# The mixing product in two halves of its sum, the first beside the masked attention

## What is computed

```python
h = rms_norm(x, mix_norm_g)
(lru_x, lru_z, ml_u, ml_o, ml_z, ml_i, ml_f,
 mo_q, mo_k, mo_v, mo_z) = jnp.split(h @ w_in, SPLIT_POINTS, axis=-1)
y_lru = rg_lru_branch(...)                      # 512 wide
y_ml = mlstm_branch(...)                        # 768 wide, 4 heads
# masked attention, 6 heads of 128, with linear biases; 768 wide
y_mo = softmax(q k^T * scale - slope * distance, causal) v * silu(mo_z)
x = x + concatenate([y_lru, y_ml, y_mo]) @ w_out        # the mixing product
x = x + memory_cross_attention(rms_norm(x), rms_norm(mem))
```

## Time and profile before

| what | value |
|---|---|
| median of 3 runs | 1984.25 us (1982.85 to 1990.74) |
| the profiled execution's own time | 1982.04 us |
| its span, first to last instruction | 1980.2 us |
| mean granted TensorE clock | 0.953 |
| busy: PE, PEld | 1813.0, 1547.3 us |
| busy: DVE, ACT | 1434.6, 805.5 us |
| read from memory | 307 MB, 156 GB/s over the span |

### The profile page before, as it was taken

How to read it: one execution, slowest core, us unless ns; L and a number is a source line. 1 busy time by engine, 2 the same in 40 slices (tenths; PEclk the granted TensorE clock), 3 DMA queues, 4 the chain that set the end, 5 groups by cost and what they waited for, 6 DMA issues and landing times. The chain is left out here.

```text
span 1980.2 us, 26887 instructions
## 1 busy us (share of the span) xinstructions
PE 1813.0 (92%) x10559; PEld 1547.3 (78%) x10559; DVE 1434.6 (72%) x2250; ACT 805.5 (41%) x1268; POOL 7.2 (0%) x18
## 2 busy tenths in 40 slices
PE   7999988997799887999999989997989999999797
PEld 6899988885688766878887867785978976666597
DVE  5788768787799767878687869776772677777444
ACT  6544364634244534233332223223453444444343
POOL 1000000000000000000000000000000000000000
PEclk9999999997899888999999999998999999999898
DMA  6588745443577333345454546552342443433252
GB/s 211 188 263 264 234 127 160 128 133 119 188 247 255 128 108 117 106 160 177 132 197 158 194 131 214 188 191 91 121 150 74 142 165 114 139 111 114 73 184 89
DMA packets 168998, 311.09 MB, mean 157 GB/s; under 512 B 14908, under 2 KB 23464, under 8 KB 168872
## 3 DMA queue, kind: packets, MB, share of 16 engines
q1 hardware_dynamic: 162176, 305.70, 47.2%
q10 hardware_dynamic: 6248, 3.62, 0.6%
q0 software_dynamic: 448, 0.06, 0.0%
HBM read 307.23 MB, written 2.10 MB: 156 GB/s over the span
## 5 line engine op out<-in xcount | busy, mean ns | idle before, releaser
L489 PE MATMUL bank<-operand,w_high 128*128 128x256 f32 (+1 forms) x2720 | 875.4, 322 | 58.2 <-DVE w_low L307 30.2
L490 PE MATMUL bank<-operand,w_high 128*128 128x256 f32 (+1 forms) x2720 | 863.4, 317 | 0.0
L491 PE MATMUL bank<-operand,w_low 128*128 128x256 f32 (+1 forms) x2720 | 862.8, 317 | 0.0
L489 PEld LDWEIGHTS bank<-operand,w_high 128*128 128x128 f32 x2720 | 528.6, 194 | 119.1 <-DVE w_low L307 34.9
L307 DVE TENSOR_TENSOR w_low<-raw,w_high 128x1024 fp32r<-128x1024 f32 (+4 forms) x416 | 455.8, 1129 | 218.0 <-ACT w_high L297 216.2
L297 ACT ACTIVATE w_high<-raw 128x1024 fp32r<-128x1024 f32 (+4 forms) x416 | 395.4, 981 | 467.7 <-PE bank L491 252.5
L490 PEld LDWEIGHTS bank<-operand,w_high 128*128 128x128 f32 x2720 | 528.6, 194 | 30.8
L491 PEld LDWEIGHTS bank<-operand,w_low 128*128 128x128 f32 x2720 | 527.9, 194 | 31.2
L422 DVE SCALAR_TENSOR_TENSOR ada_acc<-ada_raw,silu_c,ada_acc 128x512 f32<-128x512 f32 x720 | 489.7, 747 | 6.6 <-DMA ada_raw<-in_ada_w 4.5
L489 PE MATMUL bank<-operand_small,w_high 128*128 128x512 f32 (+1 forms) x320 | 124.9, 390 | 11.6 <-DVE big L405 5.4
L490 PE MATMUL bank<-operand_small,w_high 128*128 128x512 f32 (+1 forms) x320 | 120.9, 378 | 0.0
(11 more groups left out here) (347 smaller groups left out, 1375.0 us busy)
## 6 DMA issues: line engine op xcount, KB each, us to landing
ada_raw<-in_ada_w SPq DMA_DIRECT2D x192, 512.0 KB, 4.0
raw<-in_w_in SPq DMA_DIRECT2D x96, 512.0 KB, 4.8
raw<-in_pool_w_in SPq DMA_DIRECT2D x64, 512.0 KB, 5.2
raw<-in_mla_w_in SPq DMA_DIRECT2D x48, 512.0 KB, 4.5
raw<-in_w_out SPq DMA_DIRECT2D x32, 512.0 KB, 6.1
raw<-in_pool_w_out SPq DMA_DIRECT2D x32, 512.0 KB, 5.8
raw<-in_mla_w_out SPq DMA_DIRECT2D x32, 512.0 KB, 4.6
raw<-in_xa_wkv SPq DMA_DIRECT2D x16, 512.0 KB, 4.5
```

Source lines behind the costliest of these rows:

```text
L489: pe.matmul(out_, hi, x[:, 0, :], start=first, stop=False, skip_group_check=True)
L490: pe.matmul(out_, hi, x[:, 1, :], start=False, stop=False, skip_group_check=True)
L491: return pe.matmul(out_, lo, x[:, 0, :], start=False, stop=last, skip_group_check=True)
```

## The change

The mixing product is cut in two Products over its inner dimension: `mixa` takes chunks 0 and 1 of each group (operand tiles 0 to 7), `mixo` chunks 2 and 3 (tiles 8 to 15). Both add into the residual. `mixa` runs directly behind the input product, in the stage middle, and the masked attention is written between its eight chunks in new functions, one or two steps of a head after each chunk. The stages middle, moba and mixo run into each other with no barrier. The mixing product's 28 units, the attention's four and the eight of `win_c` are dealt anew: 14 in `win_c`, 10 in `mixa`, 16 in `mixo`. Values are turned and copied two heads at a time. `mixo` has two units a chunk, and the steps beside it (turns, context sums, operands) are packed two to a chunk. The old branches for the masked attention in `pe_attn`, `act_attn` and `dve_attn` go. Cut to what matters:

```diff
-    mixo = Product("mixo", w_out, 4, 4, 4, 1, "add1", half=1, dest=0, banks=5)
+    mixa = Product("mixa", w_out, 2, 4, 4, 1, "add1", half=1, dest=0, korder=[0, 1], banks=4)
+    mixo = Product("mixo", w_out, 2, 4, 4, 1, "add1", half=1, dest=0, korder=[2, 3], banks=5)
...
-              win_c: {divmod(c, 4): 1 for c in (3, 8, 9, 10, 11, 21, 22, 23)},
-              mixo: {(i, j): 2 if j else 1 for i in range(4) for j in range(4)}}
+              win_c: {divmod(c, 4): n for c, n in ((3, 1), (7, 1), (8, 1), (9, 1), (10, 2), (11, 1), (12, 1), (15, 1),
+                                                   (21, 2), (22, 2), (23, 1))},
+              mixa: {(i, j): 2 if (i, j) in ((0, 0), (3, 1)) else 1 for i in range(4) for j in range(2)},
+              mixo: {(i, j): 2 for i in range(4) for j in range(2)}}
     UNITS, unit = {}, 0
     for p in products:
-        keys = [("moba", 0, h) for h in range(4)] if p is mixo else []
-        for key in keys + [(p.name, i, j) for i in range(p.groups) for j in range(p.chunks)]:
-            n = 1 if key in keys else SPARSE[p].get(key[1:], 0) if p in SPARSE else ada.get(p, 0)
+        for key in [(p.name, i, j) for i in range(p.groups) for j in range(p.chunks)]:
+            n = SPARSE[p].get(key[1:], 0) if p in SPARSE else ada.get(p, 0)
             UNITS[key] = list(range(unit, unit + n))
             unit += n
...
-        PRIMED = {"front": [win_c], "moba": [mixo], "cross": [xo], "pairs": [mo]}
+        PRIMED = {"front": [win_c], "cross": [xo], "pairs": [mo]}
...
+            pe.wait_ge(split_lo, splits["lru"] + 4)
+            for c in range(8):
+                i, j = divmod(c, 2)
+                pe_chunk(pe, mixa, i, j, slab_after(mixa, i, j))
+                pe_moba(pe, c)
 
         def act_middle(act):
             for c in range(24):
...
                 if j == 0 and i:
                     act_evac(act, win_c, i - 1)
                 act_beside(act, c)
-            act_evac(act, win_c, 5)
+            for c in range(8):
+                act_high(act, mixa, *divmod(c, 2))
+                if c == 0:
+                    act_evac(act, win_c, 5)
+                act_moba(act, c)
+            act_high(act, mixo, 0, 0)
+            act_moba(act, 8)
...
+            for c in range(8):
+                i, j = divmod(c, 2)
+                dve_low(dve, mixa, i, j)
+                if i and j == 0:
+                    dve_evac(dve, mixa, i - 1)
+                dve_moba(dve, c)
+                dve_ada(dve, mixa, i, j)
+            dve_low(dve, mixo, 0, 0)
+            dve_evac(dve, mixa, 3)
+            dve_moba(dve, 8)
...
+            def scores(h):
+                if h:
+                    mb_dve.wait(pe, "l", h - 1)
+                for qt in range(2):
+                    ins = pe.matmul(PB[5][:, qt * T:(qt + 1) * T], tile(MQ[h])[:, qt * P:(qt + 1) * P], tile(MK[h]),
+                                    start=True, stop=True)
+                mb_pe.inc(ins, "s", h)
...
+            def turn_probs(h):
+                mb_dve.wait(pe, "nr", h, 1)
+                if h:
+                    mb_act.wait(pe, "pt", h - 1)
+                else:
+                    mb_act.wait(pe, "v", 0)
...
+            def output(h):
+                mb_act.wait(pe, "pt", h)
+                if h:
+                    mb_dve.wait(pe, "o", h - 1)
...
+            if c == 0:
+                pe.wait_ge(act_freed, win_c.free0 + 24)
+                mf_dve.wait(pe, "y", 5)
+                turn_values(0)
+                turn_values(1)
+                scores(0)
+            elif c == 1:
+                turn_values(2)
+                scores(1)
+                turn_probs(0)
+            elif c < 6:
+                scores(c)
+                turn_probs(c - 1)
+                output(c - 2)
+            elif c == 6:
+                turn_probs(5)
+                output(4)
+            else:
+                output(5)
...
+            def exponentials(h):
+                mb_dve.wait(act, "nm", h)
+                if h >= 2:
+                    mb_pe.wait(act, "t", h - 2)
+                for qt in range(2):
+                    mb_act.inc(s(ML(h)[:, qt, :], ML(h)[:, qt, :], ACT.Exp, bias=mb_stat(h)[:, qt:qt + 1], scale=scale_o,
+                                 accum_out=mb_stat(h)[:, 2 + qt:3 + qt]), "e", h, qt)
...
+            def probs(h):
+                mb_pe.wait(act, "t", h)
+                if h >= 2:
+                    mb_pe.wait(act, "o", h - 2)
+                mb_act.inc(s(MP(h).rearrange("p a t -> p (a t)"), PB[6][:, :], ACT.Copy), "pt", h)
...
+            elif c == 1:
+                values(0)
+                values(1)
+                exponentials(0)
+            elif c == 2:
+                values(2)
+                probs(0)
+                exponentials(1)
+            elif c < 7:
+                probs(c - 2)
+                exponentials(c - 1)
+            elif c == 7:
+                probs(5)
+                for h in range(4):
+                    mb_dve.wait(act, "o", h)
+                    act_split(act, "mo", h, tile(MZ[h]), mo_operand(h, 0))
...
+            def maxima(h):
+                mb_pe.wait(dve, "s", h)
+                if h >= 2:
+                    mb_pe.wait(dve, "t", h - 2)
+                st.inc(v.scalar_tensor_tensor(ML(h), DIST, sl[h] / scale_o, PB[5][:, :].rearrange("p (q t) -> p q t", q=2),
+                                              ALU.mult, ALU.add), "l", h)
+                st.inc(v.tensor_reduce(mb_stat(h)[:, 0:2], ML(h), AX.X, ALU.max), "mx", h)
+                st.inc(v.tensor_scalar(mb_stat(h)[:, 0:2], mb_stat(h)[:, 0:2], -scale_o, None, ALU.mult), "nm", h)
...
+            def probs(h):
+                mb_act.wait(dve, "e", h, 1)
+                st.inc(v.reciprocal(mb_stat(h)[:, 2:4], mb_stat(h)[:, 2:4]), "rs", h)
+                for qt in range(2):
+                    st.inc(v.tensor_scalar(ML(h)[:, qt, :], ML(h)[:, qt, :], mb_stat(h)[:, 2 + qt:3 + qt], None, ALU.mult),
+                           "nr", h, qt)
...
+            if c == 0:
+                for h in range(6):
+                    mb_z.wait(dve, "z", h)
+                    mb_zz.inc(v.tensor_tensor(tile(MZ[h]), tile(MZ[h]), tile(O + h), ALU.mult), "z", h)
+                dve.wait_ge(dist_in, 16)
+            elif c < 7:
+                maxima(c - 1)
+                if c >= 4:
+                    output(c - 4)
+                probs(c - 1)
+            elif c == 7:
+                output(3)
+            else:
+                output(4)
+                for h in range(4):
+                    dve_split(dve, "mo", h, tile(MZ[h]), mo_operand(h, 1), mo_operand(h, 0))
...
+            for c in range(8):
+                i, j = divmod(c, 2)
+                if c < 2:
+                    pe.wait_ge(split_lo, splits["mo"] + (2, 6)[c])
+                pe_chunk(pe, mixo, i, j, slab_after(mixo, i, j))
+                if 1 <= c <= 4:
+                    pe_turn(pe, 2, 2 * c - 2)
+                    pe_turn(pe, 2, 2 * c - 1)
+                if c >= 6:
+                    context(2 * c - 12)
+                    context(2 * c - 11)
+                if i and j == 1:
+                    sums(i - 1)
...
+            act.wait_ge(split_lo, splits["mo"] + 6)
             sp_turn(act, 2, a["ctx_2"][0])
...
+            for c in range(8):
+                i, j = divmod(c, 2)
+                if c:
+                    act_high(act, mixo, i, j)
+                if c == 7:
+                    act_rows(act, 0, 8)
+                if 2 <= c <= 5:
+                    act_turn(act, 2, 2 * c - 4)
+                    act_turn(act, 2, 2 * c - 3)
+                if c >= 6:
+                    act.wait_ge(tr_free, 24)
+                    for q in (2 * c - 12, 2 * c - 11):
                         ctx_act.inc(s(SQK[q], quarter(CT0, q), ACT.Square), "s", q)
-                    if i and j == 1:
-                        operand(i - 1)
+                if i and j == 1:
+                    operand(i - 1)
...
+            for c in range(8):
+                i, j = divmod(c, 2)
+                if c:
+                    dve_low(dve, mixo, i, j)
+                if i and j == 0:
+                    dve_evac(dve, mixo, i - 1)
+                if i and j == 1:
+                    operand(i - 1)
+                dve_ada(dve, mixo, i, j)
...
-        STAGES = ["front", "middle", "moba", "mixo", "cross", "xo", "latents",
+        STAGES = ["front", "middle", "mixo", "cross", "xo", "latents",
                   "pairs", "mo"]
...
-                if name != "mo":
+                if name not in ("middle", "mo"):
                     stage_end(eng, me)
...
-            for h in range(4):
-                if h in (0, 2):
-                    sp_chunk(sp, mixo, 0, h // 2)
-                sp_unit(sp, UNITS["moba", 0, h][0])
-            for i in range(4):
-                for j in range(4):
-                    if (i, j) not in ((0, 0), (0, 1)):
```

(36 more changed lines are left out.)

77 lines of the change are left out of this document (41 added, 36 removed).

## The result

| | before | after |
|---|---|---|
| median of 20 runs each, side by side | 1983.31 us | 1991.58 us (1986.46 to 1994.39) |
| ratio, with its 95% interval | | 1.0038 (1.0029 to 1.0046) |
| profiled execution, its span | 1982.04, 1980.2 us | 1994.39, 1992.6 us |
| busy: PE, PEld | 1813.0, 1547.3 us | 1814.2, 1553.5 us |
| busy: DVE, ACT | 1434.6, 805.5 us | 1440.1, 805.1 us |

The forecast was 1978.0 us, the range 1965 to 1986. The change made the kernel 8 us slower, about 0.4%: still within half a per cent of no change, but outside the range and on the other side. The profiled execution of the changed kernel is the slowest of its twenty, so some 2 to 3 us of what its trace shows are not in the median; 1.5 us more than in the trace before lie ahead of input chunk 0 (259.82 in place of 258.31 us), where the code is the same.

The account below looks back on a forecast made before the run. VectorE was taken as the bound, only its waits removable: new waits 20.5 against old 24.5 (-4.0), absorbed upstream -8.1, added work +5.3, tail +0.6, together -6.2 us; from the median 1984.25 to 1978.0, range 1965 to 1986.

Parts of the forecast that it names:

- Step 7: Mixing product's second half: two units a chunk, operand steps 1.6 us of work, waits 1.4 (bytes), 1.1 to 3.1 (slab 7), 1.5 (late loads).
- Step 8: Tail after the last mixing chunk: 3.4 us more TensorE sums, mostly under VectorE's units, so the query product starts 0.6 us later.
- Step 4: Eight chunks beside the attention: VectorE bounds at 9.6 us a head, exponentials wait 8.6 us, outputs from the third head inside that.
- quarter of the evacuation: VectorE's average share per head of emptying a group's banks beside the attention, priced at 0.67 us.
- Step 6: First half's chunk 4, where unit 47 closes slab 5: VectorE waits 2 to 4 us; gates at the start cost 0.8.
- Step 1: Input product, one more unit each in chunks 7, 10, 12, 15 and 21: 13.3 us added, 8.1 absorbed in VectorE's waits.
- Step 2: Input chunk 22, where unit 40 opens a new slab and waits for slab 4: 2.4 to 3.8 us.
- Steps 3 and 5: First half may start before any head is done, two barriers vanish; its separate residual write adds 16 additions, 5.3 us on VectorE.
- A: Rival: upstream waits all absorbed (-11.3 us), no clock dips, slab 5 and late loads free; -19 us, 1965; chance 0.23.
- B: Rival: loads become the bound, four of eight new two-unit chunks wait 1.5 us more each; 1984, no change; chance 0.16.
- C: Rival: TensorE's clock stays at its lower level through the attention, 6.4 us more a head; 2016; chance 0.09.
- over 3 us a head: Sign in the attention: if VectorE waits this long, exponentials are queued behind ScalarE's wait for the previous head's turned probabilities.

Follow-up runs that it names:

- e12_only: The changed kernel with only ScalarE's operand step and TensorE's residual sums put ahead of the turned context's copies, turns and sums: 1979.45 us, ratio 0.9970 to the old kernel.
- e3_both: The changed kernel with heads' outputs one step earlier and a unit between each head's maxima and normalisation: 1977.77 us, ratio 0.9970 to the old kernel.
- e5_order: e3_both with ScalarE's operand step ahead of context copies and squares, and TensorE's residual sums ahead of turns and context sums: 1969.54 us, ratio 0.9932.
- e11_slabs: The old kernel with 14 units in the input product, no slab's last unit sharing a chunk with the next slab's first: 1984.78 us, ratio 0.9998.
- e8_all: e3_both with the edits of e5_order, e6_deal23 and e7_slab together: 1963.38 us, ratio 0.9902 to the old kernel.
- e7_slab: e3_both with a slab's two matmuls behind their chunk's last tile, in the mixing product only: 1972.11 us, ratio 0.9945 to the old kernel.
- e6_deal23: e3_both with unit 40 in chunk 23 of the input product in place of chunk 22: 1974.78 us, ratio 0.9964 to the old kernel.

## Why the prediction was wrong, step by step

The bound was named correctly: VectorE, not TensorE's hole of 53 us. The failure lies in the list of its waits: 20.5 us were expected, 30.6 are in the list, and 4.8 more in the tail. Between the two profiled executions the time grew by 12.4 us where 6.2 less were forecast. Of these 18.6 us, 1.5 lie before input chunk 0, 3.3 upstream of chunk 22, 10.5 between chunk 22 and the query product, 2.8 in its first two chunks, and 0.5 behind. The 10.5 are almost all waits. Against the middles of the prediction's terms they are 4.6 more at the operand steps, 2.7 at the banks, 2.6 at the scores, 1.2 each at slab 4 and for bytes, and 2.2 less elsewhere. The median missed by 13.6; it was forecast from the 1984.25 us of three runs, and twenty gave 1983.31.

- **Step 7, the main failure.** "Operand steps" were priced by their 1.6 us of work, with no wait. The prediction followed ScalarE's loads and SyncE's order, but not the two turns that ScalarE now issues ahead of each operand step, nor the sums behind two context sums. Measured: waits of 4.6 and 4.8 us, and part of the 4.8 at the banks. Undone, 13.5 us go (e12_only, 9 to 17 by the intervals); behind e3_both the same edit gave 7.5 (e5_order), so it is the largest of the failed terms, but its size hangs on what stands ahead of it.
- **Step 8.** The tail was priced at +0.6. TensorE does the 3.4 us of extra sums as said, but the last operand step waits for them; the time from the query product's chunk 0 to chunk 2 grew from 13.2 to 16.5 us.
- **Step 4.** The exponentials were right: 8.4 us, six waits, the first 2.71 of which the table load has 1.28; the Trainium skill's ScalarE: Activation LUTs, Rules for kernel authors would have made that first wait 1.4 us longer, and the trace does not agree with it here. Wrong was that a head's output "lies inside the wait" and costs nothing else. It releases bank 7 a step too late, 11.6 us of TensorE's time, worth 2.6 us as the change stands and 5.4 once the exponentials are covered. (The "quarter of the evacuation" in this step is half of its 1.33 us; the 0.67 used is right.)
- **Step 6.** Slab 5 was put at 2 to 4 us and the scores waited 5.6 with both causes in the same chunk; with the output out of the way 3.8 were left, inside the bounds.
- **Step 1.** Of 13.3 us 4.8 were absorbed in the profiled execution, where chunk 22 came 8.5 us late, and 4.7 to 7.4 over the other traces with these units before it (5.9 to 8.6 late), not 8.1. The two added units of chunks 10 and 12 disappeared as said: from chunk 10 to 15 it took 45.7 us before and 46.1 after. That of chunk 7 was paid in full, its step growing from 10.1 to 12.7 us, as the wait for the mLSTM scores moved along with TensorE. That the work moved away is a full gain downstream was not true for the old kernel either (e11_slabs).
- **Step 2.** 4.3 us, against 2.4 to 3.8. Taking it away shortened the stretch by 3.3.
- **Steps 3 and 5** hold: no wait at the start of the first half, and 32 additions in place of 16, of 0.41 us each.

**Rivals.** A (the waits fold away, 1965) is wrong for the change. e8_all, with 1963, shows that such a time was there to be had, once the order was mended. B: one wait of 2.6 us for bytes; loads were not it. C: the granted clock was 0.94 in the first half (0.93 from 470 to 570 us), under the 0.95 I had named and far from 0.6. TensorE did idle beside most heads, and single chunks ran partly at the lower of the two levels:

```profile
506.08 0.36 PE L491 MATMUL bank<-operand,w_high 128*128 128x256 f32 x1 [4.03 <-DVE big L401]
...
507.28 0.41 PE L491 MATMUL bank<-operand,w_high 128*128 128x256 f32 x1
...
509.81 0.28 PE L491 MATMUL bank<-operand,w_high 128*128 128x256 f32 x1
```

The 0.41 us matmuls step by 0.21 us, those of 0.28 by 0.12. The short step was back 3.7 us after the gap, and the chunk took 7.5 us in place of 6.0. Behind the longest stop, 5.46 us, the granted clock was 0.50 from 528.2 to 532 us, and the short step was back at 533.8. The clock thus went down and up again, and did not stay down between heads, as this rival's price assumed. The Trainium skill's TensorE: Matmul & The Clock Gate, A second HAM failure mode: psum-queue depth-cycling, says of such stops that the clock swings between its two levels, not that it stays at the lower; in that the trace agrees. The dips went when the waits went (0.98 in e3_both's first half). That they cost only where VectorE waits for the chunk is argued, not measured.

The chance of 0.09 for slower was put on C alone. No rival stood for order: a step queued behind another engine's later work. The sign that the text itself named (over 3 us a head) looked at the exponentials only.

What stays open: why e12_only gained some 2 us more than one trace shows (11.6 us), how its gain divides between the two engines, where most of e7_slab's 5.0 us lies, and the size of e6_deal23.

## What to carry to other kernels

When steps beside a product are packed two to a chunk, write each engine's new order side by side and ask of every step what stands ahead of it in its own queue and who releases its buffer: the busy time stays the same, and the order alone was worth 27 us here, between 1991.6 and 1963.4. A buffer with one slot that is emptied one step late turns a step of slack into a wait on the other engine: 11.6 us of TensorE's time here, and 2.6 to 5.4 us of the whole. And a wait that one has priced is also a place: put independent work there before counting it as a cost.

## What the runs showed that I had not expected

Gains of several edits to the order were close to additive, even more than additive for bank 7 and the exponentials. Each wait taken away could have uncovered the next instead, as e3_both's rival had it. And a gap on TensorE does not always cost pace. These two rows of its timeline begin a chunk each:

```profile
475.22 0.39 PE L491 MATMUL bank<-operand,w_high 128*128 128x256 f32 x1 [1.89 <-DVE w_low L309]
...
494.30 0.38 PE L491 MATMUL bank<-operand,w_high 128*128 128x256 f32 x1 [3.05 <-DVE w_low L309]
```

The first, behind the shorter gap, took 7.5 us to its last matmul (482.72), the second 6.0 (500.31). The chunk ahead of the first had itself begun behind a gap of 3.3 us; the one ahead of the second had not. Whether that is the reason was not tried.
